# Attention of a hybrid encoder block: values stationary on two column halves, y kept by channels with one norm per half, scores four ahead, half of loop 2's copies on ScalarE

## The chip, the cores and the metric

One core of one Trainium2 chip runs the kernel. The metric is the device time of one execution in microseconds (us), the median of the runs. Names of engines: PE is TensorE (matmuls), PEld its weight loads, DVE is VectorE, ACT is ScalarE, POOL is GpSimd, SP is SyncE, which issues most DMAs.

## The reference

```python
h = adaln_pre(x, g_norm[l, 0], shift[:, 0], scale[:, 0])
x = x + FFN_RES * (1.0 + gate[:, 0])[:, None, :] * swiglu(h, w_ffn1_in[l], w_ffn1_out[l])
h = adaln_pre(x, g_norm[l, 1], shift[:, 1], scale[:, 1])
proj = h @ w_in                      # q, k, v, xc, gate_b, gate_c
q, k = rms_norm(q, q_norm_g), rms_norm(k, k_norm_g)        # per head, 64 channels
s = q @ k.T * HEAD_DIM ** -0.5 + bias                      # own chunk and the 8 before it
y_attn = softmax(s) @ v
y_conv = gate_b * causal_depthwise_conv(gate_c * xc, w_conv, b_conv)
y = concatenate([rms_norm(y_attn, g_attn_out), rms_norm(y_conv, g_conv_out)])
x = x + (1.0 + gate[:, 1])[:, None, :] * (y @ w_out)
h = adaln_pre(x, g_norm[l, 2], shift[:, 2], scale[:, 2])
x = rms_norm(x + FFN_RES * (1.0 + gate[:, 2]) * swiglu(h, w_ffn2_in[l], w_ffn2_out[l]), g_final[l])
```

Sizes: 1024 tokens, 1024 channels, 8 heads of 64 channels, 2816 hidden channels in each feed-forward part, all float32.

## The kernel before, in words

The program is one long list of instructions for each engine, written out by hand; engines meet by semaphores alone (`wait_ge`, `then_inc`), and each engine keeps its own order. It runs a feed-forward part, then the mixer twice (`mx` 0 for tokens 0 to 511, `mx` 1 for tokens 512 to 1023), then the second feed-forward part. Large products are made of three passes over split operands (a `hi` and a `lo` part; `passes`, L2679 to L2681, and `more`, L2685 to L2687). The change touches only the mixer's attention.

In each half of the mixer, after the projections and beside the last gate products (`gate_mm`), runs the attention loop, here called loop 1 (`mx` 0) and loop 2 (`mx` 1). It has 32 units `s`: four query tiles of 128 tokens (`qt = s // 8`) times eight heads. A unit sees `nb` key tiles of 128 keys: 4, 3, 2, 1 for the four query tiles of loop 1 (it goes backwards), always 5 in loop 2. The steps of a unit:

- S, scores (PE L3094, two heads at once, on the upper and the lower 64 rows of the array). DVE adds the bias and takes the minimum (L2526); ACT takes the exponential and the row sum (L1598, and a small read of the accumulator).
- T (PE L3109): `nb` transposes of the probabilities into PSUM. DVE copies them to SBUF (L2540). In loop 2 there is one PSUM place for them, so the next T waits for the copy.
- V, values (PE L3128): for each key tile the transposed probabilities (128 keys by 128 queries) are the weights, and 64 columns of `v` pass through. A float32 matmul shows as two records, each with its own weight load.
- After the eighth head of a query tile: DVE multiplies by the inverse row sums (L2554) into `ytok`, which is tokens by channels; ACT squares (L1605), DVE and POOL make the norm's factor (L2563, L1002), DVE applies it with the row of gains (L2569), PE transposes the tile (L3138), ACT and DVE split it into `y_hi` and `y_lo` (L1614, L2581).

The order on PE in each unit is T(s), then S of two units for every even s (four units ahead in loop 1, two in loop 2), then V(s-1). Between them lie, in loop 1, six output products of 12 passes each (`OUT_FILL`, 128x512), and the statistics of the convolution's norm (`norm_stats`, L2708, and `norm_spread`, L2730), for which ACT squares four tiles (L1582) and POOL adds them (L1009). After loop 1 come two more such products with the last transpose of y between them, then the attention's part of the output product; after loop 2 eight such products, then that part. Two query tiles have PSUM banks 7 and 6 in turn for y.

Of the kernel before, what the change touches and what calls it, by code (L numbers as in the profile page):

```python
# [106 lines left out]
SM_BADA, SM_GN, SM_GF, SM_QG, SM_KG, SM_WC, SM_BC, SM_GC, SM_C = 0, 72, 96, 104, 105, 106, 118, 122, 126  # L107
SM_COLS = 134
# [12 lines left out]
def build(nc, xT, w_ada, c_row, small, w_f1i, w_f1o, w_mix, w_mo, w_f2i, w_f2o, bias_ext, g_attn, out):  # L121
# [31 lines left out]
    o = R_S + 1056  # L153
# [17 lines left out]
    few = tiny("few", 4)  # L171
    ssum, yvar, yr, qg = (few[:, i:i + 1] for i in range(4))
# [41 lines left out]
    ytok = at("ytok", DA, F32, R_HID + 80 * KB)  # L214
    g_row = at("g_row", DA, F32, R_HID + 82 * KB)
# [3 lines left out]
    s_sb = at("s_sb", 2 * BANDW, F32, R_H + 20 * KB)  # L219
    pT = at("pT", 2 * BANDW, F32, R_H + 25 * KB)  # L220
# [3 lines left out]
    q_norm = [qrow, ytok]  # L224
# [15 lines left out]
    with ctx:  # L240
# [5 lines left out]
        def y_bank(qt):  # L246

            return bank[7 - qt % 2]
# [93 lines left out]
        grow_in = sem("grow_in")  # L342
# [6 lines left out]
        pt_done = sem("pt_done")  # L349
        pv_mm = sem("pv_mm")  # L350
        rrec_done = sem("rrec_done")
        yt_done = sem("yt_done")
        ysq_done = sem("ysq_done")
        yvar_done = sem("yvar_done")
        ypow_done = sem("ypow_done")
        yn_done = sem("yn_done")
        yT_mm = sem("yT_mm")
        ya_hi_done = sem("ya_hi_done")
# [21 lines left out]
        OUT_SPLITS = [{6: 0, 7: 1, 10: 2, 12: 3, 20: 4, 24: 5, 29: 6}, {1: 0, 2: 1, 7: 2, 10: 3}]  # L380

        OUT_CONV = (2, 3, 4, 5, 6, 7, 0, 1)
        OUT_FILL = (17, 19, 21, 23, 25, 28)
# [15 lines left out]
        def s_buf(mx, s, n):  # L399

            if mx == 0:
                return col(k_sb, s % 4 * S + T, n)
            return col(s_sb, s % 2 * BANDW, n)

        def p_buf(mx, s, n):

            if mx == 0:
                return col(v_sb, (TT + s % 4) * DA, n)
            return col(pT, s % 2 * BANDW, n)
# [9 lines left out]
        def bias_count(mx, n):  # L419

            return HEADS + 2 * n if mx else n

# [179 lines left out]
        def _(sp):  # L602
# [201 lines left out]
            def mix_loads(mx):  # L804
# [27 lines left out]
                if mx == 0:  # L832
                    g0 = bass.AP(g_attn.tensor, 0, [[0, P], [1, DA]])
                    sp.dma_start(g_row[:], g0).then_inc(grow_in, 16)
# [47 lines left out]
        def _(pool):  # L882
# [87 lines left out]
            for mx in range(2):  # L970
# [28 lines left out]
                def y_power(qt):  # L999

                    pool.wait_ge(yvar_done, TT * mx + qt + 1)
                    nc.gpsimd.tensor_tensor(yr[:], yvar[:], mhalf[:, 0:1], ALU.pow).then_inc(ypow_done, 1)  # L1002
# [8 lines left out]
                def conv_lo(ct):  # L1011

                    pool.wait_ge(y_hi_done, KA * mx + ct + 1)
# [6 lines left out]
                if mx == 0:  # L1020
# [4 lines left out]
                    y_power(0)  # L1025
                    conv_lo(1)
                    conv_lo(2)
                    conv_lo(3)
                    out_lo(2)
                    out_lo(3)  # L1030
                    y_power(1)
                    out_lo(4)
                    out_lo(5)
                    y_power(2)
                    out_lo(6)
                    y_power(3)
                else:
# [5 lines left out]
                    y_power(0)  # L1043
                    conv_lo(0)
                    conv_lo(1)
                    y_power(1)
                    conv_lo(2)
                    conv_lo(3)
                    y_power(2)
                    y_power(3)  # L1050
# [17 lines left out]
        def _(act):  # L1068
# [328 lines left out]
            for mx in range(2):  # L1397
# [202 lines left out]

                def y_square(qt):
                    n = TT * mx + qt
                    act.wait_ge(yt_done, n + 1)
                    act.wait_ge(yvar_done, n) if n else None
                    nc.scalar.activation(sq[:], ytok[:], ACT.Square, accum_out=ssum[:]).then_inc(ysq_done, 1)  # L1605

                def y_split(qt):
                    n = TT * mx + qt
                    act.wait_ge(yT_mm, n + 1)
                    yb = y_bank(qt)  # L1610
# [76 lines left out]
        def _(dve):  # L1687
# [539 lines left out]
            for mx in range(2):  # L2227
# [314 lines left out]
                def y_rows(qt):  # L2542
# [8 lines left out]
                    if n:  # L2551
                        dve.wait_ge(yT_mm, n)
# [760 lines left out]
```

## Time and profile before

| | us |
|---|---|
| median of 3 runs | 1804.15 |
| lowest, highest | 1803.94, 2211.68 |
| span of the profiled execution, first to last instruction | 1802.4 |
| median less that span | 1.75 |
| PE busy in the span | 1774.5 |

The profiled execution has no total of its own beside its span; the 1.75 us stand for what lies around it. The highest run lies far from the two others and is not used. Times in the trace count from the first instruction. The time of a matmul in the trace includes its way through the array, so the step from one start to the next, and not the duration, tells what a matmul costs in a stream.

### The profile page before, as it was taken

The numbers are of one execution on the slowest core, as the hardware profiler recorded it, in microseconds if no ns is written. First come the engines' busy times: TensorE is split into PE (matmuls) and PEld (weight loads), VectorE is DVE, ScalarE is ACT, GpSimd is POOL, SyncE is SP. The second block draws the span as 40 slices with busy tenths as digits, with TensorE's granted clock in tenths as the row PEclk, the third lists the DMA queues.
The fourth block names the chain that finished last, engine by engine and source line by source line (L and its number), as shares of the span: only waits on it lengthen the run. The fifth ranks groups of instructions, "written<-read, shape, count | busy, mean of one in ns | idle before, by whom it ended". The sixth has DMA issues, their size and how long they took to land.

```text
span 1802.4 us, 21397 instructions
## 1 busy us (share of the span) xinstructions
PE 1774.5 (98%) x8316; PEld 1466.4 (81%) x8316; DVE 1181.8 (66%) x1380; ACT 683.3 (38%) x875; POOL 492.9 (27%) x274
## 2 busy tenths in 40 slices
PE   6999999999999999999999999999999999999997
PEld 5888888888888888877788888888888888888886
DVE  7987766767787575456676576685544444577756
ACT  4442333333334452325444353353233333333442
POOL 1044556644100000205211230333445433310000
PEclk9999999999999999999999999999999999999998
DMA  8146655556956335431244311303422333585633
GB/s 351 42 152 213 225 169 169 191 192 228 345 192 239 99 106 179 142 100 59 88 136 150 117 48 43 122 1 125 137 88 89 99 109 118 193 302 193 228 93 117
DMA packets 87107, 269.89 MB, mean 150 GB/s; under 512 B 8304, under 2 KB 8432, under 8 KB 85488
## 3 DMA queue, kind: packets, MB, share of 16 engines
q1 hardware_dynamic: 82848, 261.20, 42.7%
q10 hardware_dynamic: 4176, 7.60, 1.1%
q8 instruction: 50, 0.82, 0.2%
q14 instruction: 33, 0.27, 0.1%
HBM read 215.81 MB, written 52.95 MB: 149 GB/s over the span
## 4 chain that ended last, share of the span: by engine, by line
PE 92%; issue 3%; DVE 3%; DMA 1%; ACT 1%; POOL 0%; DVEq 0%; SPq 0%; POOLq 0%; ACTq 0%
PE pair L2685 23%; PE pair L2687 23%; PE pair L2686 23%; PE pair L2679 5%; PE pair L2681 5%; PE pair L2680 5%; PE pair L3128 3%; PE pair L3094 2%; PE pair L3109 1%; DMA raw<-w_mix 1%; DVE acc L1825 1%; DVE cb L1863 0%; PE pair L2782 0%; PE pair L2708 0%; PE pair L2730 0%
## 5 line engine op out<-in xcount | busy, mean ns | idle before, releaser
L2685 PE MATMUL pair<-cb,w_hi 128*128 128x512 f32 x864 | 336.3, 389 | 0.8 <-DVE w_lo L1698 0.6
L2686 PE MATMUL pair<-cb,w_hi 128*128 128x512 f32 x864 | 336.1, 389 | 0.0
L2687 PE MATMUL pair<-cb,w_lo 128*128 128x512 f32 x864 | 336.1, 389 | 0.0
L2685 PE MATMUL pair<-h_hi,w_hi 128*128 128x512 f32 x824 | 321.9, 391 | 2.3 <-DVE h_lo L1835 2.3
L2687 PE MATMUL pair<-h_hi,w_lo 128*128 128x512 f32 x824 | 321.1, 390 | 0.0
L2686 PE MATMUL pair<-h_lo,w_hi 128*128 128x512 f32 x824 | 321.1, 390 | 0.0
L2685 PEld LDWEIGHTS pair<-cb,w_hi 128*128 128x128 f32 x864 | 162.2, 188 | 35.5 <-DVE w_lo L1698 1.0
L2687 PEld LDWEIGHTS pair<-cb,w_lo 128*128 128x128 f32 x864 | 162.2, 188 | 33.7
L2686 PEld LDWEIGHTS pair<-cb,w_hi 128*128 128x128 f32 x864 | 162.2, 188 | 33.4
L2685 PEld LDWEIGHTS pair<-h_hi,w_hi 128*128 128x128 f32 x824 | 155.1, 188 | 34.6 <-issue 2.1
L2687 PEld LDWEIGHTS pair<-h_hi,w_lo 128*128 128x128 f32 x824 | 154.9, 188 | 32.4
L2686 PEld LDWEIGHTS pair<-h_lo,w_hi 128*128 128x128 f32 x824 | 155.1, 188 | 32.1
L1708 DVE TENSOR_TENSOR w_lo<-a,w_hi 128x1024 fp32r<-128x1024 f32 x84 | 97.4, 1159 | 84.0 <-ACT w_hi L1129 83.8
L1698 DVE TENSOR_TENSOR w_lo<-s_w,w_hi 128x1024 fp32r<-128x1024 f32 x60 | 93.5, 1559 | 88.0 <-ACT w_hi L1099 88.0
L1129 ACT CAST w_hi<-a 128x1024 fp32r<-128x1024 f32 x84 | 82.1, 978 | 179.0 <-PE pair L2687 169.6
L901 POOL TENSOR_TENSOR rinv<-var,mhalf 128x4 f32<-128x4 f32 x10 | 13.8, 1379 | 482.5 <-DVE var L1738 482.5
L1698 DVE TENSOR_TENSOR w_lo<-ga,w_hi 128x1024 fp32r<-128x1024 f32 x64 | 90.5, 1415 | 84.1 <-ACT w_hi L1099 84.0
L912 POOL TENSOR_TENSOR s_w<-ua,ua 128x1024 f32<-128x1024 f32 x19 | 56.9, 2994 | 236.6 <-issue 216.0
L1724 DVE TENSOR_TENSOR w_lo<-raw,w_hi 128x1024 fp32r<-128x1024 f32 x59 | 72.3, 1228 | 73.0 <-ACT w_hi L1153 72.7
L1099 ACT CAST w_hi<-s_w 128x1024 fp32r<-128x1024 f32 x60 | 63.2, 1053 | 144.0 <-PE pair L2687 93.7
L1153 ACT CAST w_hi<-raw 128x1024 fp32r<-128x1024 f32 x70 | 73.0, 1046 | 97.9 <-PE pair L2681 67.9
L1802 DVE CUSTOM_DVE_ANT_0 ada_w<-ada_w,s_row 128x1024 f32<-128x1024 f32 x56 | 90.0, 1606 | 0.0
(274 smaller groups left out, 3239.5 us busy)
## 6 DMA issues: line engine op xcount, KB each, us to landing
raw<-hs SPq DMA_DIRECT2D x70, 512.0 KB, 3.7
ada_w<-w_ada SPq DMA_DIRECT2D x56, 512.0 KB, 3.8
raw<-w_mix SPq DMA_DIRECT2D x46, 512.0 KB, 3.6
hs<-tt SPq DMA_DIRECT2D x20, 1024.0 KB, 6.4
a<-w_f1o SPq DMA_DIRECT2D x30, 512.0 KB, 6.3
a<-w_f2o SPq DMA_DIRECT2D x30, 512.0 KB, 6.0
ga<-w_f1i SPq DMA_DIRECT2D x22, 512.0 KB, 4.3
ua<-w_f1i SPq DMA_DIRECT2D x22, 512.0 KB, 4.4
```

The costliest lines, as they stand in the source:

```text
L1129: nc.scalar.copy(col(w_hi, out_slot(F, q) * CW, w), col(src, a, w)).then_inc(w_hi_done, 1)
L1153: nc.scalar.copy(col(w_hi, mix_slot(n) * CW, CW), raw_chunk(n)).then_inc(w_hi_done, 1)
L1698: nc.vector.tensor_tensor(col(w_lo, o, CW), src[:], col(w_hi, o, CW).bitcast(F32), ALU.subtract).then_inc(w_ready, 1)
L1708: nc.vector.tensor_tensor(col(w_lo, o, w), col(src, a, w), col(w_hi, o, w).bitcast(F32), ALU.subtract).then_inc(w_ready, 1)
L1724: nc.vector.tensor_tensor(col(w_lo, o, CW), raw_chunk(n), col(w_hi, o, CW).bitcast(F32), ALU.subtract).then_inc(w_ready, 1)
L1802: nc.vector.tensor_tensor_reduce(out=tile, in0=tile, in1=row, scale=1.0, scalar=0.0, op0=ALU.mult, op1=ALU.add, accum_out=mod[:, f:f + 1]) ...
L2679: nc.tensor.matmul(dst, lh, rh, start=first, stop=False)
L2680: nc.tensor.matmul(dst, lh, rl, start=False, stop=False)
L2681: return nc.tensor.matmul(dst, ll, rh, start=False, stop=last)
L2685: nc.tensor.matmul(dst, lh, rh, start=first, stop=False, skip_group_check=True)
L2686: nc.tensor.matmul(dst, lh, rl, start=False, stop=False, skip_group_check=True)
L2687: return nc.tensor.matmul(dst, ll, rh, start=False, stop=False, skip_group_check=True)
```

## The change

V now takes 64 columns of `v` as the weights and passes the 128 columns of transposed probabilities through. The two heads of a pair are written to partitions 0 to 63 and 64 to 127 of one bank (7), key tile by key tile in turn. So y comes out as channels by tokens. The inverse row sums are spread by ACT over 64 columns a head, transposed by PE (in the place of the transpose of y), copied by ACT, and multiplied in by DVE (`ya`). The squares go by ACT to `ysq`, are added by POOL, and the norm over channels is made once per half: a product with ones for four tiles, one power, one spread over the columns. The gains are applied by channel in four steps of 512 columns, and four splits follow, all behind the loop. Loops are written in rounds of two units. Loop 2's scores run four ahead, its probabilities have four buffers on either side, and the copies of its even units are ACT's. One output product of loop 1 (it was at s = 28) stands behind the loop.

```diff
-        CONV_STATS, CONV_SPREAD = (5, 6), (7, 8)
+        CONV_STATS, CONV_SPREAD = (5, 5), (7, 7)
-        OUT_FILL = (17, 19, 21, 23, 25, 28)
+        OUT_FILL = (17, 19, 21, 23, 25)
-        AHEAD = (4, 2)
+        AHEAD = 4
+        ROUNDS = UNITS // 2
+        def by_act(mx, s):
+            return mx == 1 and s % 2 == 0
...
+                def y_sum(qt):                       # POOL
+                    n = TT * mx + qt
+                    c = tile_at(mx, qt) * P
+                    pool.wait_ge(y_act, 3 * n + 3)
+                    nc.gpsimd.tensor_tensor(ysq[:, 0:2 * P], ysq[:, 0:2 * P], ysq[:, 2 * P:4 * P],
+                                            ALU.add).then_inc(yacc_done, 1)
+                    pool.wait_ge(yacc_done, 2 * n + 1)
+                    nc.gpsimd.tensor_tensor(yacc[:, c:c + P], ysq[:, 0:P], ysq[:, P:2 * P],
+                                            ALU.add).then_inc(yacc_done, 1)
...
+                def act_copy(s):                     # ACT
+                    act.wait_ge(t_mm, g + 1)
+                    if s >= 4:
+                        act.wait_ge(pv_mm, (g - 4) // 2 + 1)
+                    nc.scalar.copy(p_buf(mx, s, nb * P), t_buf(mx, s, nb * P)).then_inc(pa_done, 1)
+                def r_expand(qt):
+                    nc.scalar.copy(ysq[:].rearrange("p (h d) -> p h d", h=HEADS), rb).then_inc(y_act, 1)
+                def r_copy(qt):
+                    act.wait_ge(y_mm, y_step(mx, qt))
+                    nc.scalar.copy(ysq[:], bank[R_BANK][:]).then_inc(y_act, 1)
+                early = AHEAD if mx == 0 else 2
...
+                def y_mul(qt):                       # DVE
+                    dve.wait_ge(y_act, 3 * n + 2)
+                    dve.wait_ge(pv_mm, (UNITS * mx + HEADS * (qt + 1)) // 2)
+                    nc.vector.tensor_tensor(dst, turned(bank[Y_BANK]), turned(ysq[:]), ALU.mult).then_inc(yt_done, 1)
...
+                for r in range(ROUNDS):
+                    s = 2 * r
+                    if s % HEADS == HEADS - 2:
+                        y_recip(s // HEADS)
+                    if not by_act(mx, s):
+                        probs(s)
+                    probs(s + 1)
+                    if s >= HEADS and s % HEADS == 0:
+                        y_mul(s // HEADS - 1)
+                    if s + AHEAD < UNITS:
+                        scores(s + AHEAD)
+                        scores(s + AHEAD + 1)
+                    extras(s)
+                    extras(s + 1)
+                y_mul(TT - 1)
+                if mx == 0:
+                    x_conv(5)
+                y_mean()
+                y_gain(0)
+                y_gain(1)
+                y_low(0)
+                y_gain(2)
+                y_low(1)
+                y_gain(3)
+                y_low(2)
+                y_low(3)
...
-                        mm = nc.tensor.matmul(y_bank(qt)[:, h * HD:(h + 1) * HD],
-                                              p_buf(mx, s, nb * P)[:, a * P:(a + 1) * P],
-                                              v_sb[:, kt * DA + h * HD:kt * DA + (h + 1) * HD],
-                                              start=(a == 0), stop=(a == nb - 1))
+                        for e in range(2):           # PE, value_pair
+                            h = 2 * hp + e
+                            mm = nc.tensor.matmul(bank[Y_BANK][e * HD:(e + 1) * HD, hp * P:(hp + 1) * P],
+                                                  v_sb[:, kt * DA + h * HD:kt * DA + (h + 1) * HD],
+                                                  p_buf(mx, s + e, nb * P)[:, a * P:(a + 1) * P],
+                                                  start=(a == 0), stop=(a == nb - 1))
...
+                for r in range(ROUNDS):              # PE
+                    s = 2 * r
+                    prob_mm(s)
+                    if mx == 0:
+                        prob_mm(s + 1)
+                    if s >= HEADS and s % HEADS == 0:
+                        rrec_turn(s // HEADS - 1)
+                    if r:
+                        value_pair(r - 1)
+                    if mx == 1:
+                        prob_mm(s + 1)
+                    between(s)
+                    between(s + 1)
+                    if s + AHEAD < UNITS:
+                        score_pair(s + AHEAD)
+                rrec_turn(TT - 1)
+                value_pair(ROUNDS - 1)
                 if mx == 0:
-                    for i in (6, 7):
+                    for i in (5, 6, 7):
                         pe.wait_ge(xc_done, i - 1)
-                        out_part(OUT_CONV[i], 0, FILL_BANK[i % 2], True, False)
+                        out_part(OUT_CONV[i], 0, FILL_BANK[i % 2], True, i == 5)
+                        if i == 5:
+                            attn_stats()
                         if i == 6:
-                            y_turn(TT - 1)
+                            attn_spread()
```

In the diff above a comment names the engine of a function; `attn_stats` is four float32 products of 128x128 by one column, `attn_spread` four transposes of 128x128. After loop 2 they stand behind the second and the third of the eight products. The load of the row of gains (`g_row`, one DMA) goes; the gains ride with the small parameters.

## Rows read from the trace of the kernel before

**Rows 1.** The page: span, busy time and share of the engines, chain by engine.

```profile
span 1802.4 us, 21397 instructions
PE 1774.5 (98%) x8316; PEld 1466.4 (81%) x8316; DVE 1181.8 (66%) x1380; ACT 683.3 (38%) x875; POOL 492.9 (27%) x274
...
PE 92%; issue 3%; DVE 3%; DMA 1%; ACT 1%; POOL 0%; DVEq 0%; SPq 0%; POOLq 0%; ACTq 0%
```

**Rows 2.** Windows over both loops: stretch, length, busy us (instructions) by engine, clock, DMA.

```profile
806.90:822.50 15.60, 15.37 (x117) 11.88 (x115) 11.29 (x27) 8.29 (x19) 6.22 (x6) 1.00 0.00 1
822.50:836.50 14.00, 12.35 (x97) 9.71 (x96) 12.01 (x32) 10.80 (x26) 8.96 (x6) 1.00 0.24 76
836.50:868.00 31.50, 30.70 (x185) 24.46 (x184) 17.60 (x60) 12.51 (x36) 12.73 (x8) 1.00 0.22 67
...
1028.70:1046.30 17.60, 17.49 (x137) 14.12 (x136) 12.12 (x23) 10.40 (x20) 8.58 (x13) 1.00 0.27 89
1046.30:1107.50 61.20, 60.98 (x491) 51.91 (x491) 47.41 (x92) 28.84 (x62) 14.67 (x11) 1.00 0.09 27
```

**Rows 3.** Timeline of PE, one round of loop 2 (start us, us, operation, xcount).

```profile
1073.34 0.74 PE L3109 MATMUL pair<-ident,s_sb 128*128 128x128 f32 x5
1074.00 1.35 PE L3094 MATMUL pair<-k_sb,q_sb 64*128 64x512 f32 x8
1075.28 1.33 PE L3128 MATMUL pair<-v_sb,pT 128*128 128x64 f32 x10
1076.45 0.72 PE L3109 MATMUL pair<-ident,s_sb 128*128 128x128 f32 x5
1077.00 1.23 PE L3128 MATMUL pair<-v_sb,pT 128*128 128x64 f32 x10
1078.17 0.73 PE L3109 MATMUL pair<-ident,s_sb 128*128 128x128 f32 x5
1078.84 1.35 PE L3094 MATMUL pair<-k_sb,q_sb 64*128 64x512 f32 x8
```

**Rows 4.** Timeline of the same round, weight loads.

```profile
1076.34 0.59 PEld L3109 LDWEIGHTS pair<-ident,s_sb 128*128 128x128 f32 x5
1076.89 1.20 PEld L3128 LDWEIGHTS pair<-v_sb,pT 128*128 128x128 f32 x10
```

**Rows 5.** Groups by line and form, whole span: V and T.

```profile
L3128 PE MATMUL pair<-v_sb,pT 128*128 128x64 f32 x320 | 40.7, 275 | 0.2 <-ACT rstd L1166 0.2
L3109 PE MATMUL pair<-ident,s_sb 128*128 128x128 f32 x160 | 23.3, 276 | 0.1
L3128 PE MATMUL pair<-v_sb 128*128 128x64 f32 x160 | 23.0, 275 | 0.7 <-DVE v_sb L2540 0.5
L3109 PE MATMUL pair<-ident,k_sb 128*128 128x128 f32 x80 | 14.2, 275 | 0.0
```

**Rows 6.** Groups by line, window 1046.3 to 1107.5 of loop 2: DVE and ACT.

```profile
L2540 DVE COPY pT<-pair 128x640 f32<-128x640 f32 x25 | 20.5, 822 | 9.3 <-PE pair L3109 9.0
L1598 ACT ACTIVATE s_sb<-s_sb,nmax 128x640 f32<-128x640 f32 x23 | 19.1, 829 | 29.7 <-DVE nmax L2526 29.6
L2526 DVE CUSTOM_DVE_ANT_0 s_sb<-pair,bias 128x640 f32<-128x640 f32 x23 | 18.8, 818 | 2.9 <-PE pair L3094 2.9
```

**Rows 7.** Timeline of PE in loop 1: statistics, S behind a wait, one output product.

```profile
817.69 1.00 PE L2708 MATMUL pair<-one,acc 128*128 128x1 f32 x8
...
822.19 0.60 PE L2730 MATMUL pair<-ident,rinv 128*128 128x128 f32 x4
...
833.76 0.70 PE L3094 MATMUL pair<-k_sb,q_sb 64*128 64x256 f32 x4 [1.12 <-DVE nmax L2526]
...
838.98 0.48 PE L2679 MATMUL pair<-y_hi,w_hi 128*128 128x512 f32 x1
...
841.82 0.38 PE L3109 MATMUL pair<-ident,k_sb 128*128 128x128 f32 x2
```

**Rows 8.** Timeline of POOL: last additions of the squares in loop 1 and in loop 2.

```profile
815.12 1.27 POOL L1009 TENSOR_TENSOR acc<-acc,qsq 128x512 f32<-128x512 f32 x1
...
1039.65 1.27 POOL L1009 TENSOR_TENSOR acc<-acc,qsq 128x512 f32<-128x512 f32 x1 [0.84 <-ACT qsq L1582]
```

**Rows 9.** Timeline behind loop 1: the tail of the norm of y and its transpose.

```profile
870.44 0.54 POOL L1002 TENSOR_TENSOR few<-few,mhalf 128x1 f32<-128x1 f32 x1 [0.97 <-DVE few L2563]
871.02 0.75 DVE L2569 SCALAR_TENSOR_TENSOR ytok<-ytok,few,g_row 128x512 f32<-128x512 f32 x1 [0.66 <-POOL few L1002]
871.83 0.66 PE L3138 MATMUL pair<-ident,ytok 128*128 128x128 f32 x4 [0.84 <-DVE ytok L2569]
```

More of the change, by code:

```diff
@@ L118, in norm_acc, with build @@
     return sum(1 + t for t in NORM_TILES[2:n])
[L121 removed]
+def build(nc, xT, w_ada, c_row, small, w_f1i, w_f1o, w_mix, w_mo, w_f2i, w_f2o, bias_ext, out):
     hs = nc.dram_tensor("hs", (STEPS, P, HW), F32, kind="Internal").ap()
@@ L170, in build @@
     scol = tiny("scol", KD)
-    few = tiny("few", 4)
-    ssum, yvar, yr, qg = (few[:, i:i + 1] for i in range(4))
+    avar = tiny("avar", TT)
+    ainv = tiny("ainv", TT)
+    qg = tiny("qg", 1)
     assert base + top[0] <= nc.sbuf_usable_end, (base + top[0], nc.sbuf_usable_end)
@@ L1635, in _ @@
                         conv_part(CONV_SPLIT[mx].index(s))
+                r_copy(TT - 1)
                 y_square(TT - 1)
-                y_split(TT - 1)
+                if mx == 0:
+                    mix_hi(b + MIX_CHUNKS[mx] + 6)
+                for ct in range(KA):
+                    y_split(ct)
                 if mx == 0:
@@ L2601, in x_out, with extras @@
                         .then_inc(x_done, 1)
-                for s in range(AHEAD[mx]):
-                    scores(s)
-                for ct in range(KA):
-                    conv_gate(ct)
-                for s in range(UNITS):
-                    probs(s)
-                    if s + AHEAD[mx] < UNITS:
-                        scores(s + AHEAD[mx])
+                def extras(s):
                     if s == CONV_STATS[mx]:
@@ L3097, in score_pair, with copied @@
                                 mm.then_inc(s_mm, 1)
+                def copied(s):
+                    if by_act(mx, s):
+                        pe.wait_ge(pa_done, act_copies(s))
+                    else:
+                        pe.wait_ge(pt_done, dve_copies(mx, s))
                 def prob_mm(s):
@@ new lines, in attn_stats, with attn_spread @@
+                def attn_stats():
+                    pe.wait_ge(yt_done, TT * (mx + 1))
+                    pe.wait_ge(yacc_done, 2 * TT * (mx + 1))
+                    for t in range(TT):
+                        mm = nc.tensor.matmul(bank[R_BANK][:, t:t + 1], yacc[:, t * P:(t + 1) * P], one2[:, 0:1],
+                                              start=True, stop=True)
+                    mm.then_inc(y_mm, 1)
+                def attn_spread():
+                    pe.wait_ge(ypow_done, mx + 1)
+                    for t in range(TT):
+                        r = ainv[:, t:t + 1]
+                        src = bass.AP(r.tensor, r.offset, [list(r.ap[0]), [0, P]])
+                        mm = nc.tensor.transpose(bank[R_BANK][:, t * P:(t + 1) * P], src, ident[:])
+                    mm.then_inc(y_mm, 1)
@@ L3170, in out_part @@
                     pe.wait_ge(w_ready, n + 1)
-                    pe.wait_ge(yc_ready, KA * (mx + 1)) if part == 0 else pe.wait_ge(ya_ready, TT * (mx + 1))
+                    if part == 0:
+                        pe.wait_ge(yc_ready, KA * (mx + 1))
                     for e in range(KA):
+                        if part == 1 and m == 0:
+                            pe.wait_ge(ya_ready, KA * mx + e + 1)
                         k = (KA, 0)[part] + e
@@ L3176, in out_part, with between @@
                     mm.then_inc(w_used if m % 2 else (oc_mm, oa_mm)[part], 1)
-                for s in range(UNITS):
-                    prob_mm(s)
-                    if s % 2 == 0 and s + AHEAD[mx] < UNITS:
-                        score_pair(s + AHEAD[mx])
-                    if s:
-                        value_mm(s - 1)
+                def between(s):
                     if mx == 0 and s in OUT_FILL:
```

251 lines of the change are left out of this document (127 added, 124 removed).

## The prediction

> **What bounds the kernel now.** I read the page first [rows 1]: PE is busy for 1774.5 of 1802.4 us and holds 92% of the chain that ended last. Then the windows over the two loops [rows 2]. In loop 1 PE is nearly full, except from 822.5 to 836.5, where DVE is busy for 12.0 of 14.0 us; there a score product waits 1.12 us for DVE [rows 7], and with two smaller waits DVE sets about 1.7 us. Loop 2 is PE's alone: 61.0 of 61.2 us busy, DVE 47.4, ACT 28.8. So what PE is spared in the loops counts in full, as long as DVE and ACT keep up.
>
> What a round of two units costs PE in loop 2 is in [rows 3]: from one S to the next 4.84 us. The stream rates are in [rows 4]: five T weight loads take 0.59 us with the last one's 0.14, so (0.59 - 0.14)/4 = 0.11 us a record; ten V loads take 1.20 with the last one's 0.19, so 0.112 us a record, although only 64 columns pass. V is held by its 128-column weight load, T by either. S passes 640 columns twice for each of two heads; at T's rate of 128 columns in 0.11 us one head alone is 10 x 0.11 = 1.1 us, and both together took 1.28 with what surrounds them, so two halves of the array do run at once when they are row halves. Sum of a round: S 1.10, T 10 x 0.11 = 1.10, V 20 x 0.112 = 2.24, together 4.44. The other 0.40 us are the two changes between the whole array and row halves: 0.2 us each. T and V follow each other now without such a change.
>
> **V itself.** A key tile of a head pair is four records now, 0.448 us. After the change the weights have 64 columns and 128 columns pass, two passes for each head. If the column halves run at once, as the row halves do, it is 2 x 0.11 = 0.22 us. The records [rows 5] are 160 + 320, so 120 key tiles of pairs: 120 x (0.448 - 0.22) = 27.4 us less, 9.1 in loop 1 and 18.2 in loop 2. The bounds for the column halves: 0.22 (at once) and 0.44 (one after the other). I take 0.22, since the row halves are the nearest thing in the trace. Nor should the reading of two float32 streams be too much: such a stream passes 128 columns in 0.11 us, while the split products pass 512 in (841.82 - 838.98)/12 = 0.24 us [rows 7], nearly twice that rate.
>
> **Mode changes.** V is in column halves now, T and S are not, so V costs a change on either side. Loop 2's order is T, V, T, S: four changes a round for 13 rounds in place of two, and six more in the last two rounds and behind them: 32 more. Loop 1's order is T, T, V, S: one more a round for 13, seven more where a product, the statistics or the spread stand between V and S, six at the end: 26 more. 58 x 0.2 = 11.6 us. No row has a change into column halves. The bounds are 0.1 (only half as many weight columns have to be loaded before the first pass) and 0.3; I take 0.2, from the row halves.
>
> **The norm of y on PE.** The transposes of the inverse sums take the place of those of y, four for four: nothing. New in each half are the four products by one column, 8 records; the same statistics of the other norm show 8 in 1.00 us with about 0.25 of way through the array, so 0.86, and four transposes for the spread, 0.44 [rows 7]. 2 x 1.3 = 2.6 us. PE's sum: 27.4 - 11.6 - 2.6 = 13.2 us less.
>
> **What is late next.** A round of loop 2 becomes 1.1 + 1.1 + 1.1 + 4 x 0.2 = 4.1 us. DVE has in it two score steps and one copy, each of some 0.82 us [rows 6], 2.5; ACT has two exponentials (0.83 and 0.19 for the read) and the copy, which I take as DVE's 0.82, some 2.8. Both fit, extras too. Waits come at the edges:
> - Start of loop 2. ACT's copy of unit 0 stands ahead of the exponential of unit 2, and T(1) waits for that copy. The statistics move from s = 6 to s = 5, and POOL ends the last addition of the squares only at 1039.65 + 1.27 = 1040.9 [rows 8]; POOL must first finish the bias, which the change doesn't bring sooner, and ACT's copies now stand between its squares. Followed queue by queue, PE gets through the statistics about 2.7 us later than its own sum, and by then is where it was before at the same time.
> - End of loop 2. Without S between them T(30) waits for DVE's copy of unit 29, and the last V for that of unit 31: 0.8 + 0.5 = 1.3 us. Loop 2 has 0.6 us of waits now, so 2.7 + 1.3 - 0.6 = 3.4 more.
> - Loop 1, statistics. They stand at 817.69 now [rows 7]; PE would come to them at about 814.4, but the last addition ends at 816.4 [rows 8], perhaps 0.6 sooner: 1.4 us, and 0.9 for T(7) and for the spread behind POOL's power.
> - Loop 1, 822.5 to 836.5. PE needs about 10.6 us, DVE about 12.3: four rounds of 2.1, four steps of the convolution's norm of 0.75, `y_mul` and the reciprocal 0.9. So DVE sets it by 1.7 us, as it does now. The last small rounds wait about 1.0. New waits 2.3 + 1.7 + 1.0, less the 2.5 of now (these 1.7 and 0.8 at the end): 2.5.
> - Behind loop 1. PE now waits 0.84 us for the normed tile [rows 9]. The new chain is `y_mul`, square, two additions, statistics, power, spread: it fits behind products 5 and 6 (2.8 us each). Then come four gains, splits and subtractions, seven or eight DVE steps of 0.7 us from the spread on, while PE has only product 7 (2.8) and the first part as cover: 1.1 us. 0.3 more.
> - Behind loop 2 five of eight products (14 us) follow the spread, and nothing waits. The weights' steps queued on DVE behind it have the same 14 us of slack. If that cover were gone it would be 3 us. The removed DMA of gains costs nothing, as no wait names it; POOL's additions (8 times about 1 us) replace eight powers of 0.54 [rows 9], and it is idle for most of both loops [rows 2]. The doubled buffers cost nothing.
>
> Waits: 3.4 + 2.5 + 0.3 = 6.2. **Sum:** 13.2 - 6.2 = 7.0 us less than the profiled span of 1802.4, so a span of 1795.4; with the 1.75 us around it, the forecast is 1797 against the median of 1804.15. Measurements of this kernel tell some 2%, 36 us, from no change, so nearly every case below lies within that.
>
> **Rivals.**
> - Serial halves (chance 0.12, ends slower than now). If the column halves don't run at once, or the partitions of the output don't make them halves, a key tile is 0.44 us and V spares nothing: 120 x 0.22 = 26.4 us come back, of which about 4 fill waits. 1797 + 22 = 1819. It decides from 0.28 us a key tile on: there the whole gain is gone (7.0/120 = 0.06 above 0.22). Against it: S on row halves. For it: two streams through all 128 rows are nowhere in the trace.
> - Weight loads laid bare (0.10). T's records show a load of 0.14 us within a step of 0.11, so loads hide behind the whole array's matmuls [rows 4]. If they don't in column halves, each pass pays half of V's load step, 0.056 us: 120 x 2 x 0.056 = 13.4, less 3 that fill waits: 1807.
> - Slow hand-over (0.16). In loop 2 T(s+1) now waits for ACT's copy, and behind it V for both. If ACT, with its squares and casts between, keeps a round at 4.6 us and not 4.1, 14 rounds give back 7 us: 1804. For it: ACT takes the copy only in its turn. Against it: ACT is idle for half of loop 2, nearly all of it waiting for DVE's minima [rows 6].
> - Cheap changes (0.12): 0.1 us each, 58 x 0.1 = 5.8 less: 1791 or a little under.
>
> For the second, the Trainium skill (TensorE: Matmul & The Clock Gate, Part 3, packing small matmuls) speaks against the change: it says that a weight load overlaps running matmuls only when the row group differs, and column halves share theirs. T's rows don't agree with it for the whole array; for column halves no run here shows it yet. The same part gives 2.38 times for three column tiles, 0.79 of the ideal; an estimate from that page would make a key tile 0.22/0.79 = 0.28 us and the time 1804.
>
> **How the numbers follow.** The forecast, 1793 to 1801, has 0.46, cheap changes 0.12, slow hand-over 0.16, bare loads 0.10, serial halves 0.12, and 0.04 is for anything else, half of it a slowdown of over 2%. The range 1787 to 1811 takes in the changes' bounds (0.1 to 0.3 us, 5.8 us to either side), the hand-over and bare loads; it leaves out serial halves and the rest, and the outer ends of cheap changes. Faster by over 2% would need more than PE's whole saving without any wait (13.2): 0.01. Slower by over 2%: 0.03. Within: 0.96.
>
> **What would show it.** V's records as 128x64 weights with 128 columns, two starting within some ns of each other, pairs every 0.11 us (right) or single ones every 0.11 (serial) or pairs every 0.165 (bare loads). From S to S in loop 2 about 4.1 us. The gap from T's last start to V's first about 0.2 us over the stream. Loop 2 from 78.7 to about 71 us, loop 1 with the moved product equal to 2 us shorter, and in the waits T behind ACT's copies and the statistics behind POOL. Wrong it would be if loop 2's rounds are not set by PE, or if the time lost shows in the projections or the second feed-forward part, where I foresee no change.

## The result, and the profile after

The change makes the kernel slower: 1827.68 us (median of 4 runs, 1827.2 to 1828.22) against 1804.05 (4 runs, with the one at 2211.68), a ratio of 1.013 with a 95% interval of 1.0115 to 1.0145. That is 23.6 us more, where 7 less were forecast. The spans say the same: 1826.0 against 1802.4.

The page of the kernel after, its span, busy time and chain, against [rows 1]:

```profile
span 1826.0 us, 21464 instructions
PE 1771.9 (97%) x8340; PEld 1449.4 (79%) x8340; DVE 1163.5 (64%) x1358; ACT 699.8 (38%) x899; POOL 499.4 (27%) x284
...
PE 86%; issue 6%; DVE 3%; ACT 2%; POOL 1%; DMA 1%; SPq 0%; DVEq 0%; POOLq 0%; ACTq 0%
```

PE is busy for 2.6 us less than before, although the span is 23.6 us longer: its share of the chain falls from 92% to 86%. The time is in gaps. From the timelines, from the first T to the last V: loop 1 took 60.9 us and takes 73.0, and one output product of 2.7 us has left it; loop 2 took 78.6 and takes 80.5. Behind the last V of loop 1, up to its last product over y, it was 28.7 and is 34.7. From there to loop 2 it is 1.6 us more (132.2 and 133.8): since the scores run four ahead, a second pair of score products (at 1044.64) stands ahead of loop 2's first T, and loop 2 has one less. Behind loop 2, up to the last product over y, it was 44.0 and is 45.0. The feed-forward parts are as before within 0.5 us.

Windows of the kernel after over parts of both loops, the columns as in [rows 2]; after the "...", the windows of three of six stretches:

```profile
807.00:823.00 16.00, 13.35 (x106) 9.57 (x105) 10.39 (x26) 6.55 (x16) 6.10 (x5) 0.90 0.00 1
823.00:842.00 19.00, 12.35 (x105) 7.57 (x103) 11.96 (x35) 10.64 (x23) 8.34 (x6) 1.00 0.19 56
1065.00:1098.00 33.00, 29.99 (x296) 22.00 (x292) 19.81 (x42) 21.79 (x46) 11.20 (x8) 0.99 0.18 54
1098.00:1130.00 32.00, 24.75 (x217) 18.20 (x217) 13.50 (x28) 16.47 (x35) 5.46 (x7) 0.89 0.01 1
...
819.70:823.10 3.40, 3.40 (x24) 2.74 (x23) 2.37 (x9) 1.31 (x4) 1.02 (x1) 0.50 0.00 0
843.60:850.40 6.80, 5.35 (x24) 3.87 (x24) 1.12 (x2) 2.35 (x7) 4.17 (x3) 0.50 0.21 44
...
1099.60:1103.00 3.40, 3.40 (x14) 1.82 (x13) 0.95 (x2) 1.22 (x4) 0.34 (x1) 0.50 0.02 5
```

Two things are new. No engine fills the second window: from 823 to 842 PE is busy for 12.4 of 19 us, DVE for 12.0, ACT for 10.6. And the granted clock (the column behind POOL's) is 0.50, the lower level of 1.2 GHz, in six stretches, the third reaching behind loop 1: 819.7 (3.4 us), 843.6 (6.8), 877.7 (6.8), 1062.0, 1099.6 and 1123.5 (3.4 each), 27.2 us in all. Before the change it is 1.00 throughout the loops [rows 2].

What PE waits for, window 800 to 1140 of the kernel after (who waits, for whom: us in total, times, the longest):

```profile
PE pair L3195 <- ACT pT L1639: 10.8, 7, 3.1
PE pair L3229 <- ACT ysq L1647: 7.2, 4, 2.6
PE pair L3195 <- ACT k_sb L1629: 5.7, 3, 4.8
PE pair L2787 <- POOL acc L1038: 2.6, 1, 2.6
PE pair L3195 <- DVE pT L2603: 1.0, 1, 1.0
...
PE pair L3216 <- DVE pT L2603: 0.6, 1, 0.6
```

All such waits sum to 29.3 us; before the change the same view gives 3.2. ACT is the releaser of 23.7 us of them, and yet is busy for 38% of the span. (T is L3195 now, V L3216, S L3173; L3229 turns the spread reciprocals, L1647 is `r_expand`, L1639 `act_copy`, L1629 `softmax`.) An engine so idle is late because of the order of its queue. Three places, read off the timeline of the kernel after:

```profile
838.16 0.44 PE L3195 MATMUL pair<-ident,k_sb 128*128 128x128 f32 x2
843.41 0.56 PE L3195 MATMUL pair<-ident,k_sb 128*128 128x128 f32 x2 [4.80 <-ACT k_sb L1629]
...
841.28 1.05 ACT L1184 CAST w_hi<-raw 128x1024 fp32r<-128x1024 f32 x1 [4.07 <-DMA raw<-w_mo]
842.24 0.61 ACT L1618 CAST y_hi<-tmp 128x512 fp32r<-128x512 f32 x1
842.75 0.51 ACT L1629 ACTIVATE k_sb<-k_sb,nmax 128x256 f32<-128x256 f32 x1
...
832.71 1.28 POOL L1044 TENSOR_TENSOR y_lo<-tmp,y_hi 128x512 fp32r<-128x512 f32 x1 [3.72 <-ACT y_hi L1618]
833.94 2.37 POOL L1014 TENSOR_TENSOR w_lo<-raw,w_hi 128x1024 fp32r<-128x1024 f32 x1
```

First, loop 1. T(17) waits 4.80 us for its exponential, which stands behind the cast of output weight chunk 3 (`mix_hi`, s = 12), and that waits 4.07 us for its DMA. There are two `raw` places; the chunk's place came free only at 836.3, when POOL had subtracted chunk 1 (833.94 + 2.37), and POOL had kept that behind `conv_lo(0)`, itself late by 3.72 us. Nobody needs chunk 3 before the end of the loop.

```profile
825.52 1.03 ACT L1184 CAST w_hi<-raw 128x1024 fp32r<-128x1024 f32 x1
826.45 0.61 ACT L1629 ACTIVATE k_sb<-k_sb,nmax 128x384 f32<-128x384 f32 x1
...
827.06 0.60 ACT L1647 COPY ysq<-rrec 128x512 f32<-128x512 f32 x1
...
827.72 0.66 PE L3229 MATMUL pair<-ident,ysq 128*128 128x128 f32 x4 [2.64 <-ACT ysq L1647]
```

Second, the end of a query tile. PE waits 2.64 us for the spread reciprocals. They were ready on DVE at 820.98; ACT's queue has two exponentials and a weight cast ahead of the spread, and the first of these exponentials itself waits for scores. The same stands at 845.42 (1.45), 868.96 and 879.15.

```profile
1094.96 1.31 PE L3216 MATMUL pair<-pT,v_sb 128*64 128x128 f32 x20
1099.33 1.08 PE L3195 MATMUL pair<-ident,s_sb 128*128 128x128 f32 x5 [3.05 <-ACT pT L1639]
...
1095.86 0.75 DVE L2570 SCALAR_TENSOR_TENSOR qsq<-yc,sm,rstd 128x512 f32<-128x512 f32 x1
...
1096.64 0.62 ACT L1618 CAST y_hi<-qsq 128x512 fp32r<-128x512 f32 x1 [3.98 <-DVE qsq L2570]
1097.17 0.82 ACT L1629 ACTIVATE s_sb<-s_sb,nmax 128x640 f32<-128x640 f32 x1
...
1098.51 0.67 ACT L1639 COPY pT<-pair 128x640 f32<-128x640 f32 x1
```

Third, loop 2. ACT waits 3.98 us, with a copy queued that PE needs, for a gate tile that DVE makes at the very end of its round, behind both score steps. The copy comes 3 us late, and PE with it.

A round without such a wait, PE and one weight load of the kernel after, against [rows 3, 4]:

```profile
1089.07 1.35 PE L3173 MATMUL pair<-k_sb,q_sb 64*128 64x512 f32 x8
1090.35 0.76 PE L3195 MATMUL pair<-ident,s_sb 128*128 128x128 f32 x5
1091.05 1.31 PE L3216 MATMUL pair<-pT,v_sb 128*64 128x128 f32 x20
1092.29 0.77 PE L3195 MATMUL pair<-ident,s_sb 128*128 128x128 f32 x5
1092.99 1.35 PE L3173 MATMUL pair<-k_sb,q_sb 64*128 64x512 f32 x8
...
1091.04 1.07 PEld L3216 LDWEIGHTS pair<-pT,v_sb 128*64 128x64 f32 x20 [0.17 <-issue]
```

From S to S it is 3.92 us (4.84 before), and V of a pair with five key tiles takes 1.24 us to the next T: ten steps of 0.109 and 0.15 for the change of shape. So what the change is about works as forecast. The sum of the span: PE's work 16.1 us less (the 13.2 of the prediction and 58 x 0.05, since a change of shape costs 0.15 and not 0.2); waits 29.3 - 3.2 = 26.1 more; six stretches at half clock, in which PE is busy for 24.3 of 27.2 us; taken to do half the work there, which is an estimate, it needs 12.2 more. Together 22.2 of 23.6.

### The profile page after: what moved, and what is told of

Its sections match the earlier page's. It is cut to its first block, busy times and chain, and to the rows that moved or that the text cites. A ratio compares the mean times of both kernels' runs of the same rounds, so it can differ in the third digit from the quotient of the medians.

```text
span 1826.0 us, 21464 instructions
## 1 busy us (share of the span) xinstructions
PE 1771.9 (97%) x8340; PEld 1449.4 (79%) x8340; DVE 1163.5 (64%) x1358; ACT 699.8 (38%) x899; POOL 499.4 (27%) x284
## 4 chain that ended last, share of the span: by engine, by line
PE 86%; issue 6%; DVE 3%; ACT 2%; POOL 1%; DMA 1%; SPq 0%; DVEq 0%; POOLq 0%; ACTq 0%
PE pair L2764 22%; PE pair L2765 22%; PE pair L2766 22%; PE pair L2758 5%; PE pair L2759 5%; PE pair L2760 5%; PE pair L3173 1%; PE pair L3195 1%; PE pair L3216 1%; PE pair L2861 0%; DVE x L1888 0%; ACT w_hi L1184 0%; DVE cb L1922 0%; POOL acc L1038 0%; DVE w_lo L1757 0%
## 5 line engine op out<-in xcount | busy, mean ns | idle before, releaser
L1757 DVE TENSOR_TENSOR w_lo<-ga,w_hi 128x1024 fp32r<-128x1024 f32 x64 | 96.1, 1502 | 82.7 <-ACT w_hi L1130 82.5
```

The source lines that it names most:

```text
L1757: nc.vector.tensor_tensor(col(w_lo, o, CW), src[:], col(w_hi, o, CW).bitcast(F32), ALU.subtract).then_inc(w_ready, 1)
```

## The experiments

The first three undo one cause each. Theory Q is the order of ACT's queue; its rivals K (the clock falls by itself) and W (the wait moves on) are in the expectations. Loop lengths, waits and half-clock stretches are those of the one profiled execution of each run.

**e1_expand_early.** The spread of the reciprocals ahead of the exponential, a unit earlier.

```diff
+                    if s % HEADS == HEADS - 2:
+                        r_expand(s // HEADS)
                     if s + early < UNITS:
                         softmax(s + early)
-                    if s % HEADS == HEADS - 1:
-                        r_expand(s // HEADS)
```

> Edit: ScalarE spreads the inverse row sums (r_expand) two exponentials sooner, at s % 8 == 6 and ahead of the exponential of that unit; nothing else. Theory Q (the loss is the order of ScalarE's queue: PE waits for work that stands behind something else there, and the half-clock stretches follow from these waits): the waits of L3229 for ysq (7.2 us in four) go, about 5 us less in loop 1, and one or two of its half-clock stretches with them: 1820, between 1817 and 1823. Rival K (the clock falls by itself, since column halves and transposes are thin work for PE): the waits go but the half-clock stretches stay near 27 us: 1822 to 1824. Rival W (the queue behind is full anyway, the wait only moves to the next instruction): 1826 to 1828.

1822.23 us, 1.0095 [1.0078, 1.0112], 5.5 less than after. Waits for L1647 fall from 7.2 to 1.7 us; loop 1 takes 67.2 us instead of 73.0. Loop 2, which the edit also touches, takes 83.3 instead of 80.5, with 17 us at half clock there instead of 10.2, although its waits are the same (12.7 and 12.4 us). So the number fits Q and K alike: the waits went, and the half clock of the whole run rose from 27.2 to 30.6 us.

**e2_cast_later.** Chunk 3 cast at s = 18.

```diff
-        OUT_SPLITS = [{6: 0, 7: 1, 10: 2, 12: 3, 20: 4, 24: 5}, ...
+        OUT_SPLITS = [{6: 0, 7: 1, 10: 2, 18: 3, 20: 4, 24: 5}, ...
```

> Edit: in loop 1 ScalarE's cast of output weight chunk 3 stands at s = 18 in place of s = 12; it is not needed before the products behind the loop. Theory Q: this cast waits 4.1 us for its DMA with the exponentials of units 17 and on behind it, and T(17) waits 4.8 us; without it about 4.5 us go, and the two half-clock stretches of 6.8 us that begin at 843.6 and 877.7 shrink by at least one: 1819 to 1823. Rival K: 1822.5 to 1824, the stretches stay. Rival W: the next link (the split of the convolution's part behind VectorE) takes its place at once: 1826 to 1828.

1822.35 us, 1.01 [1.0083, 1.0116], 5.3 less. Waits of T for exponentials fall from 5.7 to 1.0 us, but those for L1647 rise to 8.4: a part came back at the next late step. Loop 1 takes 71.3 us, 1.7 less. Loop 2, which the edit doesn't touch and whose waits stay (12.8 us), takes 78.0, 2.5 less, as only 3.4 us there are at half clock. So about half of this gain isn't the edit's own. The time lies in Q's range and 0.15 below K's.

These two runs price the clock: loop 2 with the same waits has 17.1 us at half clock in e1 and 3.4 in e2, and takes 83.3 and 78.0 us, so 0.4 us are lost for each us at half clock. They also show that how much half clock follows the same waits is not fixed.

**e3_split_later.** In loop 2 the gate's splits stand two units later on ACT.

```diff
-                    if s in CONV_SPLIT[mx]:
-                        conv_part(CONV_SPLIT[mx].index(s))
+                    if s - 2 * mx in CONV_SPLIT[mx]:
+                        conv_part(CONV_SPLIT[mx].index(s - 2 * mx))
```

> Edit: in loop 2 ScalarE's splits of the convolution's part (conv_part) stand two units later in its queue than VectorE's step that feeds them. Theory Q: of the waits of T for ScalarE's copies in loop 2 (1.6, 3.3, 1.6, 3.3 us beside the split) 7 to 9 us go, and with them the half-clock stretches at 1099.6 and 1123.5 (3.4 us each, some 2 us lost): loop 2 falls from 80.5 to about 71, the time to 1818 (1816 to 1820). Rival K: the same waits go but the stretches stay: 1820 to 1821. Rival W: VectorE or POOL hands the waits on: 1826 to 1828.

1816.28 us, 1.0069 [1.0052, 1.0085], 11.4 less. Waits for ACT's copies fall from 10.8 to 2.0 us, loop 2 from 80.5 to 68.4 us, and the time is in Q's range and under K's. Two stretches of half clock there (6.8 us) are gone as well, but they were gone in e2 too, where the waits had stayed, and loop 1 has 3.4 us more of it: that this edit removed them isn't shown.

**e4_all_four.** The three together (the splits one unit later in loop 1 too), and the statistics in loop 1 one round later.

```diff
-        CONV_STATS, CONV_SPREAD = (5, 5), (7, 7)
+        CONV_STATS, CONV_SPREAD = (7, 5), (9, 7)
```

> Edit: the three before together, the splits of loop 1 one unit later too, and loop 1's statistics and spread of the convolution's norm two units later (s = 7 and 9), where the squares are summed. Theory Q: nearly all waits in the loops go and the clock stays whole: loop 1 about 57 us, loop 2 about 71: 1797 to 1803, that is what was forecast for the change. Rival K: about 10 us of half clock stay lost: 1805 to 1812. Rival W: 1815 or more.

1804.74 us, 1.0003 [0.9993, 1.0012]: 22.9 us of the 23.6 are back. That is 1.7 above Q's range, and just under K's. Loop 1 takes 62.3 us, loop 2 69.3. The waits of PE sum to 11.9 us (29.3 before these edits), and 17.0 us are at half clock (27.2): 17.4 and, by half, 5.1 us less. So the waits are the order of queues; Q's "the clock stays whole" did not come true. That e1 to e3 alone sum to 22.2 is in part chance, since the clock in loop 2 moved in e1 and e2 by itself.

**e5_pool_order.** More of it, on e4: squares of y earlier, casts and their low parts elsewhere. In loop 2, `{1: 0, 2: 1, 7: 2, 10: 3}` became `{4: 0, 6: 1, 7: 2, 10: 3}`, and on POOL `out_lo(1)` stands ahead of `conv_lo(3)`.

> The four edits of e4_all_four, and in loop 1 the sum of squares of a query tile two ScalarE units earlier, the output weights' casts 1 to 5 and their low parts on GpSimd behind the channel gate's splits and y's sum; in loop 2 the casts of the first output weights two or three units later. Theory (what is left of the loss is more of the same strict order of ScalarE and GpSimd: in e4_all_four PE still waits 1.7 and 1.6 us for the spread of the reciprocals, 1.6 us for the gate's last low part, 1.5 and 1.2 us at the start of loop 2, and runs 13.6 us at half clock behind them): 3 to 5 us of waits and 2 to 5 us of half clock go, 1796 to 1800 us, ratio 0.996 to 0.998. Rival (the waits move to the next releaser, DVE in loop 1 being the bound): 1803 to 1806, ratio 1.000.

1807.76 us, 1.0022 [1.0013, 1.0032]: both wrong. (e4 has 17.0 us at half clock, not the 13.6 of the expectation.) The first of these waits was 1.2 us in e4, the second 0.4; timeline of PE in this run:

```profile
836.36 0.77 PE L2758 MATMUL pair<-y_hi,w_hi 128*128 128x512 f32 x1 [3.00 <-POOL y_lo L1044]
...
1059.45 1.08 PE L3229 MATMUL pair<-ident,ysq 128*128 128x128 f32 x4 [5.03 <-ACT rstd L1197]
```

The first is the gate's last low part behind `out_lo(1)` on POOL. For the second, the cast of the third chunk stood ahead of the gate's `spread` on ACT and waited 3.29 us for its DMA: the fault that e2 mends, in a new place.

**e6_pe_kept_busy.** The kernel after, with transposes of the identity into a free bank ahead of four waits of loop 1. They are extra work.

```diff
+                def fill(n):
+                    for _ in range(n):
+                        nc.tensor.transpose(bank[3][:, 0:P], ident[:], ident[:])
+                    if mx == 0 and s == CONV_STATS[mx]:
+                        fill(20)
...
+                        fill(32) if s == 16 else None
                         prob_mm(s + 1)
+                        fill({8: 18, 16: 9}.get(s, 0))
```

> The kernel after the change, with TensorE turning the identity into a free bank while it waits at four places of loop 1: 20 turns ahead of the statistics (817.3, a wait of 2.65 us), 18 and 9 ahead of the spread of the reciprocals (827.7 and 845.4, waits of 2.64 and 1.45 us), 32 ahead of the seventeenth turn of probabilities (843.4, a wait of 4.8 us). It adds work that nothing uses and takes no wait away. Theory (the granted clock falls to 1.2 GHz behind idle stretches of PE): the stretches at half clock at 819.7 (3.4 us) and 843.6 (6.8 us) are gone, the first T to the last V of loop 1 takes about 68 to 70 us instead of 73.0, the kernel 1823 to 1825 us, ratio 1.010 to 1.012 against before and 3 to 5 us less than after. Rival (the clock has another cause): the stretches stay, 1827 to 1830 us.

1821.91 us, 1.0103 [1.0087, 1.0118]: 5.8 less than after, by doing more, and 1 us below what the theory gave. Windows and timeline of PE in this run (L3293 is the filling):

```profile
807.00:823.00 16.00, 15.41 (x135) 11.12 (x133) 10.31 (x28) 6.56 (x17) 6.13 (x5) 1.00 0.00 1
...
842.00:850.40 8.40, 8.26 (x53) 6.12 (x54) 2.14 (x7) 1.77 (x6) 2.77 (x2) 1.00 0.22 65
```

```profile
836.51 3.66 PE L3293 MATMUL pair<-ident 128*128 128x128 f32 x32
840.13 0.44 PE L3195 MATMUL pair<-ident,k_sb 128*128 128x128 f32 x2
```

Both stretches at 1.2 GHz are gone and loop 1 takes 68.3 us. The 10.2 us at half clock were worth 4.7 to 5.8 us, about half their length. So these two falls came from PE's standing still, and K is out for them. The third of loop 1 stays (872.8, 6.8 us); no filling stood near it, and no wait near it is over 1.7 us.

**e7_copies_on_dve.** e4 with all copies of loop 2 on DVE.

```diff
-            return mx == 1 and s % 2 == 0
+            return False
```

> e4_all_four with all copies of turned probabilities on VectorE in loop 2 too. Theory A (a round of 3.92 us is PE's: VectorE has two copies of 0.82 and two scores of 0.90, 3.45 us, ScalarE is relieved of 0.69): the clean round grows by 0 to 0.3 us, the kernel is at 1804 to 1809 us. Theory B (the half on ScalarE is what lets PE run ahead): rounds of 4.3 us or more, each with a wait of PE for pT from VectorE, 1810 to 1816 us.

1812.66 us, 1.005 [1.0035, 1.0066]: theory B, 7.9 more than e4. DVE's work fits the round, but PE now waits in nearly each one:

```profile
PE pair L3195 <- DVE pT L2603: 12.3, 15, 1.4
```

The reciprocal or a gate tile stands between the scores and the copy, and T can't go on without the copy. ScalarE's half is worth 8 us.

**e8_heads_in_turn.** e4 with the two `for` lines of V exchanged, so that the heads of a pair follow each other.

```diff
-                    for a in range(nb):
-                        kt = keys_end - nb + a
-                        for e in range(2):
+                    for e in range(2):
+                        for a in range(nb):
+                            kt = keys_end - nb + a
```

> e4_all_four with the value products of a pair one head behind the other: five (or fewer) key tiles of head e on its column half, then those of head e+1, the same instructions in another order. Theory (the halves run at once only when their products alternate, so that a key tile of a pair costs 0.22 instead of 0.44 us): 120 key tiles of pairs x 0.22 us = 26 us more where PE is the bound, in all 1820 to 1832 us, and a clean round of loop 2 of 5.0 us. Rival (a product with 64 columns of values is cheap by itself): 1804 to 1806 us.

1812.14 us, 1.0046 [1.0031, 1.0062]. Timeline of PE in this run:

```profile
1070.71 2.02 PE L3216 MATMUL pair<-pT,v_sb 128*64 128x128 f32 x20
1072.66 0.77 PE L3195 MATMUL pair<-ident,s_sb 128*128 128x128 f32 x5
```

V takes 1.95 us instead of 1.24, 0.71 more (not the 1.1 that I expected: the second head starts before the first has ended). So the theory's 1820 is missed, and the rival's 1806 too. Over 16 pairs that is 11.4 us. Loop 2 grew by 8.0: 1.4 of its waits are gone, and 3.4 us at half clock, worth 1.7.

In loop 1 I took it to cost 40 x 0.14 = 5.7 us, and the loop took 1.5 less. But the price isn't 0.14 a key tile there. V of a pair takes 1.51 us instead of 1.02 with four key tiles and 1.07 instead of 0.81 with three, and the same as before with two (0.59) and with one (0.37); the rows stand at e11. With four pairs of each that is 3.0 us. Against them stand 1.3 us of waits and 7.1 us at half clock (worth 3.5) that this run has less of in loop 1 than e4: together 1.8 less.

**e9_casts_behind.** e5 put right; the diff is against e4. In loop 2, POOL makes y's first sum ahead of `out_lo(3)`.

```diff
-        CONV_SPLIT = [(8, 10, 12, 14), ...
+        CONV_SPLIT = [(8, 9, 11, 13), ...
-        OUT_SPLITS = [{6: 0, 7: 1, 10: 2, 18: 3, 20: 4, 24: 5}, {1: 0, 2: 1, 7: 2, 10: 3}]
+        OUT_SPLITS = [{6: 0, 15: 1, 17: 2, 20: 3, 23: 4, 26: 5}, {1: 0, 4: 1, 8: 2, 11: 3}]
-                    if s % HEADS == 3 and s > HEADS:
+                    if s % HEADS == 1 + mx and s > HEADS:
                         y_square(s // HEADS - 1)
...
                     conv_lo(0)
-                    out_lo(1)
-                    conv_lo(1)
                     y_sum(0)
+                    conv_lo(1)
                     conv_lo(2)
                     conv_lo(3)
+                    out_lo(1)
```

> The four edits of e4_all_four with e5_pool_order mended where it lost: the gate's four splits at 8, 9, 11, 13 in loop 1, all four low parts and y's first sum ahead of the second output weight's low part on GpSimd (in e5_pool_order TensorE waited 3.0 us for the last of them behind it), squares of a query tile early as there; in loop 2 the casts at 1, 4, 8, 11, so that the third no longer stands ahead of the gate's spread (5.0 us in e5_pool_order). Theory (strict queue order of ScalarE and GpSimd is all that is left): against e4_all_four 3 us less waiting at 834, 837 and 867 and 2 to 5 us less half clock, 1797 to 1801 us, ratio 0.996 to 0.999. Rival (loop 1 is bound by VectorE's chain of scores, copies and splits, so that a wait removed comes back at the next turn): loop 1 from first T to last V stays at 61 to 62 us, the kernel at 1803 to 1806 us.

1798.69 us (1797.12 to 1799.31, 6 runs), 0.9967 [0.9955, 0.9979]: 5.5 less than before the change and 29 less than after. Loop 1 takes 56.6 us, loop 2 68.4. The largest waits of PE in this run, window 800 to 1140:

```profile
PE pair L3195 <- DVE v_sb L2603: 1.7, 3, 0.7
PE pair L2758 <- POOL y_lo L1044: 1.2, 1, 1.2
PE pair L3195 <- ACT pT L1639: 1.1, 2, 0.9
```

All sum to 8.6 us, and 6.8 us are left at half clock (862.9, 1043.8).

**e10_half_in_both.** e4 with ACT copying the even units in loop 1 too: `by_act` returns `s % 2 == 0`, and the counts of both copies follow.

> e4_all_four with the even copies of turned probabilities on ScalarE in loop 1 too. Theory A (loop 1's rounds without a product are bound by VectorE, 81% busy from 820 to 830 us while TensorE is 89%, and serial value products cost nothing there): VectorE gives 16 copies of 0.37 to 0.51 us to ScalarE, loop 1 (62.3 us from first T to last V) comes down by 2 to 4 us, the kernel to 1800 to 1803 us. Theory B (ScalarE's queue is the bound, it gives the spread of reciprocals and the splits late): loop 1 grows by 2 to 6 us and the waits of PE behind ScalarE grow, 1806 to 1812 us.

1805.55 us (1802.42 to 1808.65, 10 runs), 1.0007 [0.9998, 1.0017]: between the two ranges and no different from e4 beyond the noise. The profiled execution, at 1807.09, shows theory B's mechanism, loop 1 at 65.6 us (3.3 more) and PE waiting for ACT's copies there. Loop 2 was 1.4 us shorter: e4's 3.4 us at half clock there are gone, worth 1.7.

```profile
PE pair L3195 <- ACT v_sb L1639: 7.9, 6, 3.2
```

**e11_behind_in_turn.** e9 with the edit of e8.

> e9_casts_behind with the value products of a pair one head behind the other, the edit of e8_heads_in_turn. There a pair of five key tiles took 1.95 us from its first value product to the next turn of probabilities, against 1.24 in e4_all_four: 0.14 us a key tile of a pair more, and of 120 x 0.14 = 17 us only 7.4 were seen, all in loop 2 (loop 1 was even 1.5 us shorter). Theory (in loop 1 waits swallowed it; with few waits left, in e9_casts_behind 5.5 us, the dearer products show there too): loop 1 takes 2 to 5 us more than 56.6, loop 2 7 to 11 us more than 68.4, the kernel at 1808 to 1814 us. Rival (loop 1 is bound by VectorE also with its waits gone): loop 1 within 1 us of 56.6, the kernel at 1806 to 1808 us.

1808.31 us, 1.0021 [1.0011, 1.0031], 9.6 more than e9: loop 2 77.1 us (8.7 more), loop 1 57.5 (0.9 more). The time lies at the edge of both, and loop 1's length is the rival's. But its reason, a loop bound by VectorE, isn't needed. V with four and with two key tiles, PE in e9:

```profile
820.71 1.09 PE L3216 MATMUL pair<-v_sb 128*64 128x128 f32 x16
839.17 0.66 PE L3216 MATMUL pair<-v_sb 128*64 128x128 f32 x8
```

The same in this run:

```profile
821.78 1.58 PE L3216 MATMUL pair<-v_sb 128*64 128x128 f32 x16
840.50 0.66 PE L3216 MATMUL pair<-v_sb 128*64 128x128 f32 x8
```

Loop 1 has only 3.0 us of dearer V (see e8), and 1.4 us less of waits (3.1 and 4.5): 1.6 more, 0.9 measured. Loop 2 has 11.4 us of it, 0.9 less of waits and 3.4 less at half clock (1.7): 8.8 more, 8.7 measured. So the dearer V shows in full in both loops, less what the waits take in.

## Why the prediction was wrong

Forecast 1797, measured 1827.68, outside the range, and of the wrong sign.

- *V itself*: right as a price. Two column halves start 5 to 7 ns apart, and a key tile of a pair takes 0.22 us. The serial rival is out. So are bare weight loads: V's twenty take 1.07 us beside ten steps of 0.109. The Trainium skill (TensorE: Matmul & The Clock Gate, Part 3) lets a load overlap only when the row group differs; the loads of both column halves, on the same rows, don't bear that out. Its 0.79 of the ideal would be 0.28 us a key tile; the row has 0.22. That it counts in loop 1 too is borne out in e9, where the waits are small: loop 1 is 4.3 us shorter than before, 2.7 of it the moved product, and "equal to 2 us shorter" was forecast.
- *Mode changes*: right in kind, 0.15 us and not 0.2, 2.9 us to the good.
- *The norm of y and the moved product behind loop 1*: forecast 1.3 + 2.7 + 0.3 = 4.3 us; measured 6.0 with 4.1 us of it at half clock, and 5.4 in e9 with 2.9. Less half of that, both are 4.0: right.
- *What is late next*, "Both fit, extras too": the step that failed. It compared ACT's 2.8 us with a round of 4.1, and an engine's busy time says nothing of when it comes to an instruction. I followed the queues for the statistics (forecast 1.4 us, 2.65 measured) and the ends of loop 2 (start 2.7 forecast, 0.87 + 0.24 + 1.00 measured; end 1.3 forecast, 1.0 + 0.57 measured), but not for `r_expand` (four waits, 7.2 us), not for a weight cast whose DMA hangs on POOL's order (4.8), and not for the gate's splits, which DVE delivers after its scores (the greater part of 10.8). Waits were forecast 6.2 us up and are 26.1 up. The waits that went with each edit of e1 to e4 show this.
- *Slow hand-over* (0.16, 1804) was the rival nearest to it: "ACT takes the copy only in its turn". Its price was a round of 4.6 us; the rounds are 3.92, and the loss stands in seven single waits of up to 3.1 us instead. The argument against it, that ACT is idle for half of loop 2, was the error itself.
- *The clock* is in no term. Before the change PE never stood still in the loops for over 1.12 us, and the clock was 1.00; I took that as given. Its cost of 12.2 us is an estimate: half of PE's busy time in those stretches. e6 shows it for two stretches of loop 1 (10.2 us, 4.7 to 5.8 of cost), and e1 against e2 gives 0.4 us lost for each us at half clock. By these two rates 27.2 us cost 11 to 16.

Against the forecast span of 1795.4: waits 19.9 more, clock 12.2, changes -2.9, together 29.2 of 30.6. With the waits out of the way e9 runs at 1798.69, near the forecast: its arithmetic of PE held, its assumption that the other engines deliver in time didn't. That it comes so near is in part luck: its waits are 5.4 us up, near the 6.2 forecast, but its 6.8 us at half clock (some 3.4 lost, forecast at nothing) and the cheaper changes (2.9) cancel. Open is what decides whether a wait is followed by a stretch at half clock: the same waits of loop 2 came with 3.4, 10.2 and 17.1 us of it.

## What to carry to other kernels

When a step moves to an idle engine, write out that engine's queue around it: what stands ahead, and what each of those waits for. A cast for later use that waits for a DMA, or a split of something another engine makes last in its round, doesn't belong ahead of a step that the busiest engine needs. Price a wait of TensorE above its length, since slow stretches may follow it, and compare two runs only after counting those stretches in each. Measure a price on each size that the loop has: V's price at five key tiles, applied to the smaller units of loop 1, gave 5.7 us where 3.0 were. After a loss, repair the order before giving up the idea.

## What the runs showed of the hardware

- After PE had waited 4.80 us (843.41), the granted clock was 0.50 for 6.8 us; after 2.65 us at 817.33 and 3.05 at 1099.33, for 3.4. Not each wait did it: after 2.64 us at 827.72 the clock stayed at 1.00, and after 3.05 us at 1096.54 in e2 too. Nor did it take a long one: the stretch at 1062.0 has a wait of 1.00 us and the statistics' products over one column ahead of it, and no wait near that at 877.7 is over 1.7 us. A split product steps 0.43 us there (848.53 to 848.96 in the kernel after) against 0.24 [rows 7]. The Trainium skill (TensorE: Matmul & The Clock Gate, HAM oscillation) describes such falls in a kernel whose TensorE waits for DMA; here waits for ScalarE and GpSimd do it.
- Filling the waits with useless transposes made the kernel 5.8 us faster.
- Two column halves of 128 rows by 64 columns run at once when their products alternate: twenty passes in 1.09 us, start to start. One half's products behind the other's (e8, e11) cost nothing more for one or two key tiles (0.37 and 0.59 us either way), and 0.26, 0.49 and 0.71 us more for three, four and five.
- A change between the whole array and column or row halves costs 0.15 us in a round of loop 2 (four in 3.92 us).
